# Output projection with bf16 operands in its two low products, and narrow copies made by GpSimd

## The reference, cut to what matters

```python
mlstm_out = jax.nn.sigmoid(o) * ht.reshape(bsz, s, V_W).astype(x.dtype)
mix = jnp.concatenate([conv_out, mlstm_out], axis=-1)
return x + jnp.einsum('bse,ed->bsd', mix, w_out)
...
logits = jnp.einsum('nd,de->ne', tokens.astype(jnp.float32), w_router.astype(jnp.float32))
affinity = jax.nn.softmax(logits, axis=-1)
gate, idx = lax.top_k(affinity.T, cap)
```

## Time and profile before

| | |
|---|---|
| runs of the kernel before | 1306.22, 1306.37, 1306.75 us; median 1306.37 |
| span of the profiled execution | 1307.2 us |
| TensorE busy | 1253.9 us, 96% |
| VectorE busy | 905.7 us, 69% |
| ScalarE busy | 742.0 us, 57% |
| GpSimd busy | 325.7 us, 25% |
| mean granted TensorE clock | 0.984 of full speed |
| the three products of L1965 | 66.7, 62.5 and 62.7 us busy, 160 matmuls each |

### The profile page before, as it was taken

The page is one execution under the profiler, slowest core; times in us unless marked ns, Lnnn a source line. Parts: engine busy times, 40 slices in busy tenths (PEclk is TensorE's granted clock), DMA queues, the critical chain, the costliest instruction groups (busy, mean ns, idle before and its releaser), DMA issues.

```text
span 1307.2 us, 25113 instructions
## 1 busy us (share of the span) xinstructions
PE 1253.9 (96%) x9762; PEld 1029.6 (79%) x9814; DVE 905.7 (69%) x1298; ACT 742.0 (57%) x1079; POOL 325.7 (25%) x316
## 2 busy tenths in 40 slices
PE   7999999999999999779999999999999999999992
PEld 6868986666687888568988898888888888888881
DVE  6462122541586655978888888888888889888985
ACT  7645322222345544447667766776676677667762
POOL 2512221010143231141133213221323132313040
PEclk9999999999999999989999999999999999999996
DMA  8231544361188763388999999999999999999894
GB/s 268 70 116 55 167 140 136 107 180 37 61 256 236 226 211 114 115 312 269 336 305 313 321 334 298 316 324 331 299 310 327 330 298 312 326 331 297 294 372 182
DMA packets 242032, 314.76 MB, mean 241 GB/s; under 512 B 16096, under 2 KB 206048, under 8 KB 241968
## 3 DMA queue, kind: packets, MB, share of 16 engines
q1 hardware_dynamic: 226576, 268.54, 62.2%
q0 software_dynamic: 15392, 45.36, 11.8%
HBM read 274.41 MB, written 39.44 MB: 240 GB/s over the span
## 4 chain that ended last, share of the span: by engine, by line
PE 89%; DMA 4%; DVE 3%; ACT 2%; issue 2%; SPq 1%; POOL 0%; DVEq 0%; ACTq 0%; POOLq 0%
PE psum L2253 23%; PE psum L2114 15%; PE psum L2260 11%; PE psum L2276 8%; PE psum L2081 8%; PE psum L1965 8%; PE psum L2294 4%; PE psum L2285 4%; PE psum L2246 1%; DMA eraw<-in_w_up_dram 1%; PE psum L2027 1%; ACT yt L1248 1%; DMA woraw<-in_w_out_dram 1%; PE psum L1987 1%; PE psum L1945 1%
## 5 line engine op out<-in xcount | busy, mean ns | idle before, releaser
L1812 DVE TENSOR_TENSOR elo<-eraw,ehi 128x2048 bf16<-128x2048 f32 x192 | 433.1, 2283 | 1.0 <-POOLq L822 1.0
L1218 ACT ACTIVATE ehi<-eraw 128x2048 fp32r<-128x2048 f32 x192 | 362.2, 1902 | 25.8 <-PE psum L2294 18.6
L2253 PE MATMUL psum<-xc,ehi 128*128 128x320 f32 x2048 | 332.4, 314 | 1.9 <-DVE xc L1817 1.9
L2253 PEld LDWEIGHTS psum<-xc,ehi 128*128 128x128 f32 x2048 | 304.2, 189 | 3.5 <-DVE xc L1817 2.3
L2260 PE MATMUL psum<-xb,elo 128*128 128x160 bf16 x2048 | 164.4, 234 | 0.0
L1825 DVE TENSOR_REDUCE gu<-psum 128x320 f32<-128x640 f32 x128 | 105.0, 820 | 82.6 <-PE psum L2260 82.5
L2260 PEld LDWEIGHTS psum<-xb,elo 128*128 128x128 bf16 x2048 | 139.0, 98 | 13.2 <-issue 0.2
L2114 PE MATMUL psum<-hn_nar,wnar 128*128 128x512 bf16 (+1 forms) x748 | 141.2, 343 | 1.2
L2276 PE MATMUL psum<-ehi,hc 128*128 128x512 f32 x512 | 132.6, 406 | 0.0
L2114 PEld LDWEIGHTS psum<-hn_nar,wnar 128*128 128x128 bf16 x768 | 73.0, 98 | 63.0 <-issue 4.5
L2276 PEld LDWEIGHTS psum<-ehi,hc 128*128 128x128 f32 x512 | 95.1, 188 | 22.2
(11 more groups left out here) (290 smaller groups left out, 1657.9 us busy)
## 6 DMA issues: line engine op xcount, KB each, us to landing
eraw<-in_w_gate_dram SPq DMA_DIRECT2D x64, 1024.0 KB, 6.3
eraw<-in_w_up_dram SPq DMA_DIRECT2D x64, 1024.0 KB, 8.9
eraw<-in_w_down_dram SPq DMA_DIRECT2D x64, 1024.0 KB, 13.3
wraw<-in_w_in_dram SPq DMA_DIRECT2D x12, 1024.0 KB, 7.5
negm<-negm_d SPq DMA_DIRECT2D x10, 512.0 KB, 7.2
acc_d<-x POOLq DMA_DIRECT2D x10, 512.0 KB, 5.4
tok_d<-tk POOLq DMA_DIRECT2D x10, 512.0 KB, 2.9
v<-v_d SPq DMA_DIRECT2D x18, 256.0 KB, 4.3
```

What stands on the lines that cost most here:

```text
L1218: act.activation(f["ehi"][:, j % RING, :], f["eraw"][:, raw_slot(s, j), :], ACT.Copy).then_inc(S["ehi"], 1)
L1812: dve.tensor_tensor(f["elo"][:, j % RING, :], f["eraw"][:, raw_slot(s, j), :], f["ehi"][:, j % RING, :].bitcast(F32), ALU.subtract).then_i ...
L2253: pe.matmul(o[:, 0:2 * NC], hi[:, k, c], x[:, k, :, :].rearrange("p a t -> p (a t)"), start=(k == 0), stop=False, skip_group_check=True)
```

## The change

The low halves and bf16 copies of the high halves now live together, in `mxn` and `won`, two bf16 planes (LOW and HIGH) in the place of the fp32r `mxl` and `wol`. VectorE's two subtractions write the LOW plane. GpSimd writes the HIGH plane: `out_weights_narrow(k)` copies a rounded weight slice (128x1024), behind the semaphore that its LOW plane has been written, because that plane's source lies in the same place; `mix_narrow(n, k0)` copies half of a tile's rounded mix (128x512), behind `mxh_done`. The high product stays fp32r; the two products with a low half take both operands in bf16. `project` gets the new waits: `wo_nar` for each k of the first tile, `mx_nar` ahead of k = 0 and of k = 4. In GpSimd's order the copies of weights 0 to 3 stand ahead of the last staging store, those of 4 to 7 between the first tile's two mix copies; in each turn one mix copy stands at the head and one behind `select_causal`.

```diff
-        for specs in ([("mxh", [P, KD, T], F32R), ("mxl", [P, KD, T], F32R)],
-                      [("woh4", [P, KD, T], F32R), ("wol4", [P, KD, T], F32R)],
+        for specs in ([("mxh", [P, KD, T], F32R), ("mxn", [P, KD, 2 * T], BF16)],
+                      [("woh4", [P, KD, T], F32R), ("won4", [P, KD, 2 * T], BF16)],
...
+            def out_weights_narrow(k):
+
+                pool.wait_ge(S["wo_lo"], k + 1)
+                pool.tensor_copy(out_narrow(k, HIGH), out_hi(k).bitcast(F32)).then_inc(S["wo_nar"], 1)
+
+            def mix_narrow(n, k0):
+
+                pool.wait_ge(S["mxh_done"], 2 * n + (1 if k0 == 0 else 2))
+                pool.tensor_copy(mxn[:, n % 2, HIGH, k0:k0 + 4, :], mxh[:, n % 2, k0:k0 + 4, :].bitcast(F32)
+                                 ).then_inc(S["mx_nar"], 1)
...
             for i in in_last[3:]:
+                if i == in_last[-1]:
+                    for k in range(4):
+                        out_weights_narrow(k)
                 store_group(i)
+            mix_narrow(0, 0)
+            for k in range(4, KD):
+                out_weights_narrow(k)
+            mix_narrow(0, 4)
             for n in range(NT + 2):
+                if 1 <= n < NT:
+                    mix_narrow(n, 0)
...
                     select_causal(n + 2)
+                if 1 <= n < NT:
+                    mix_narrow(n, 4)
...
-                dve.scalar_tensor_tensor(out_lo(k), out_raw(k), d["hgc"][:, k - 4:k - 3] if k >= 4 else 1.0,
+                dve.scalar_tensor_tensor(out_narrow(k, LOW), out_raw(k), d["hgc"][:, k - 4:k - 3] if k >= 4 else 1.0,
...
-                dve.tensor_tensor(mxl[:, s, 0:4, :], cvs[:, s, :, :], mxh[:, s, 0:4, :].bitcast(F32), ALU.subtract
+                dve.tensor_tensor(mxn[:, s, LOW, 0:4, :], cvs[:, s, :, :], mxh[:, s, 0:4, :].bitcast(F32), ALU.subtract
...
                     if n == 0:
                         pe.wait_ge(S["wo_lo"], k + 1)
+                        pe.wait_ge(S["wo_nar"], k + 1)
+                    if k0 == 0 and k == 0 and h == 0:
+                        pe.wait_ge(S["mx_nar"], 2 * n + 1)
                     if k == 4:
                         pe.wait_ge(S["mxl_done"], n + 1)
-                    xh, xl = mxh[:, n % 2, k, :], mxl[:, n % 2, k, :]
-                    wh, wl = out_hi(k)[:, c], out_lo(k)[:, c]
-                    for a, (x, w) in enumerate(((xh, wh), (xh, wl), (xl, wh))):
+                        pe.wait_ge(S["mx_nar"], 2 * n + 2)
+                    x, w = mxn[:, n % 2, :, k, :], [out_narrow(k, a)[:, c] for a in (LOW, HIGH)]
+                    for a, (x, w) in enumerate(((mxh[:, n % 2, k, :], out_hi(k)[:, c]), (x[:, HIGH, :], w[LOW]),
+                                                (x[:, LOW, :], w[HIGH]))):
```

More of the change, by code:

```diff
@@ L237, in hybrid_conv_mlstm_moe @@
         d.update(overlay(at_weights, ("woraw0", [P, 4, D], F32)))
-        d.update(overlay(at_weights, ("wol0", [P, 4, D], F32R)))
+        d.update(overlay(at_weights, ("won0", [P, 4, 2 * D], BF16)))
         d.update(overlay(at_weights + 2 * SLOT, ("woh0", [P, 2, D], F32R)))
@@ L264, in hybrid_conv_mlstm_moe @@
         mxh = d["mxh"][:, 2:4, SP_:T].rearrange("p s (k t) -> p s k t", k=KD)
-        mxl = d["mxl"][:, 0:2, SP_:T].rearrange("p s (k t) -> p s k t", k=KD)
+        mxn = d["mxn"][:, 0:2, 2 * SP_:2 * T].rearrange("p s (a k t) -> p s a k t", a=2, k=KD)
         cvs = d["cvs"][:, 1, SP_:T].rearrange("p (s k t) -> p s k t", s=2, k=4)
@@ L278, in out_hi, with out_narrow @@
             return d["woh4"][:, k, SP_:T]
-        def out_lo(k):
-            return d["wol0"][:, k, :] if k < 4 else d["wol4"][:, k, SP_:T]
+        def out_narrow(k, a):
+            return d["won0"][:, k, a * D:(a + 1) * D] if k < 4 else d["won4"][:, k, 2 * SP_ + a * D:2 * SP_ + (a + 1) * D]
         HALF2, PROMPT = 32, 64
@@ L338, in hybrid_conv_mlstm_moe @@
             "ld0 ld1 ldm0 ldm1 ld_mix0 ld_mix1 ld_x0 ld_x1 padded qs_done s_ps e_exp e_done sd_done num_ps router "
-            "den_done hb_done ht_done hsum mix_done mixT_ps mxh_done mxl_done o_ps x1_done "
+            "den_done hb_done ht_done hsum mix_done mixT_ps mxh_done mxl_done wo_nar mx_nar o_ps x1_done "
             "x1_out0 x1_out1 sum2 tk_done tk_out0 tk_out1 xT_ps2 xT_done "
@@ L1618, in heads_low @@
                 dve.wait_ge(S["mxh_done"], 2 * n + 2)
-                dve.tensor_tensor(mxl[:, n % 2, 4:8, :], psum[:, 5, :].rearrange("p (k t) -> p k t", k=4),
+                dve.tensor_tensor(mxn[:, n % 2, LOW, 4:8, :], psum[:, 5, :].rearrange("p (k t) -> p k t", k=4),
                                   mxh[:, n % 2, 4:8, :].bitcast(F32), ALU.subtract).then_inc(S["mxl_done"], 1)
```

## The result

The changed kernel takes **1321.37 us** (median of 4 runs, 1320.84 to 1322.50), the kernel before 1306.56 beside it. The ratio is 1.0115, with a 95% interval of 1.0102 to 1.0127. It is slower by 14.8 us, where I had forecast 8.0, and lies just above my range. The profiled execution has a span of 1319.2 us.

The account below looks back on a forecast made before the run. TensorE, busy for 96% of the span, was taken to bound the kernel. Start 4.1 + clock 1.4 + turn 2 1.0 + six turns 1.8 - tail 0.3 = +8.0 on 1306.4: 1314.4 us, range 1307.5 to 1320.5.

Parts of the forecast that it names:

- TensorE's gain: Output projection: triples with two bf16 products take 0.6725 instead of 0.685 us, saving 0.2 us a tile, 2.0 for ten.
- Place 1, the start: Start of the stage: TensorE waits at k = 4 for the mix cast behind the weight casts; cost 4.1 us (3.3 to 4.5).
- This alone would be harmless: Start: first four weight casts make the last staging store, first mix cast and first projection 1 to 2 us late, harmlessly.
- The clock: Start: after TensorE's idle stretches matmuls run at half speed for about 3.4 us; cost 1.4 us (0 to 2.9).
- Turn n = 2: Loop, tile 2: x has no room before the transposes, so the turn gets 1.0 us longer (0 to 1.6).
- Turns n = 3 to 8: Loop, six tiles: TensorE waits 0.35 to 0.75 us for x, less its gain: +0.3 each, 1.8 us together.
- With the two engines taking turns, two to four of the small operations each wait for a scaling: Loop: VectorE's inverse square root operations each wait for a 0.68 us GpSimd scaling; x comes 1.06 to 1.45 us late.
- or at 415.95 behind VectorE's conv subtraction: Loop: alternative start of GpSimd's four scalings, 415.95 instead of 415.45, if they wait for VectorE's conv subtraction.
- the signs that I had named: Loop: VectorE's small operations of 0.5 us or more, TensorE idle 0.3 to 0.8 at x's transposes, turns of 17.4 to 17.8.
- the whole-run hold: Loop: VectorE's chain to x held for the whole run of GpSimd's scalings, coming 1.85 us late.
- Heavier: Rival: VectorE held for the whole run of scalings, clock low for two stretches: +13.8 us, 1320.2; chance 0.15.
- Tail: Last turns, n = 9 and 10: no scalings there, so most of the gain is kept, -0.3 us.

Follow-up runs that it names:

- e3: Changed kernel without GpSimd's bf16 copies and the waits for them; TensorE takes bf16 low halves for both operands, leaving the cross products out: 1304.29 us.
- e6: e7 with ScalarE instead of GpSimd making the bf16 copies of weights 0 to 3: 1306.09 us.
- e7: e1 with GpSimd's cast of the heads half of the first mix ahead of the casts of weights 6 and 7: 1308.41 us.
- e1: Changed kernel with GpSimd's cast of the conv half of the mix behind the query scalings in the loop instead of ahead: 1312.22 us.
- e5: Changed kernel with the query scalings also waiting for VectorE's conv low halves: 1317.82 us.
- e8: Changed kernel with the conv half's cast and the DMA issue of the store of x swapped in GpSimd's loop: 1315.03 us.
- e9: Changed kernel with each of the four scalings waiting for the semaphore of the one before, leaving gaps between them: 1318.10 us.
- e4: Changed kernel with all casts kept, but TensorE using low halves for both operands and waiting for casts only at a tile's last products: 1319.48 us.
- e11: e6 with TensorE's k = 6 and 7 products last in tile 0, and ScalarE also making the copies of weights 6 and 7: 1305.75 us.

## Why the prediction was wrong, step by step

**TensorE's gain: right.** 0.2 us a tile forecast, 0.16 measured (17.24 to 17.08), with the bf16 pair at the pace I took from the input projection. The Trainium skill's 131 ns (page "TensorE: Matmul & The Clock Gate", Back-to-back issue gap), by which it would have been an estimated 30 us, doesn't hold in this kernel: e3 wins 1.8.

**Place 1, the start: right mechanism, 1.15 us short.** TensorE resumes at 386.47 where 387.5 less 2.09, 385.4, was forecast. The failed step is "This alone would be harmless", on the first four weight casts. I moved them in time only, and did not ask which operation of VectorE's they lie beside. They held the mix for 4.53 us, and with it the store and the low halves, and e6 against e7 puts 2.3 us on it.

**The clock: right**, 1.6 us in the changed kernel's trace (24 matmuls in 7.1 us instead of 5.5) against 1.4. It varies: e1, e5 and e8 have the same wait of 4.3 us but 6.8 us at half clock instead of 3.4, and e1's start is 1.1 us longer. 2.9 had been my upper bound.

**Turn n = 2: right**, +1.17 against +1.0, by the mechanism I named. Its scalings follow at 404.03, behind `conv_low`, and three small operations wait:

```profile
404.92 0.57 DVE L1346 TENSOR_SCALAR ms<-ms 128x5 f32<-128x5 f32 x1 [0.72 <-DVE nlm L1654]
405.52 0.64 DVE L1347 TENSOR_SCALAR ms<-ms 128x5 uint32<-128x5 uint32 x1
406.20 0.65 DVE L1350 TENSOR_TENSOR ms<-ms 128x5 f32<-128x5 f32 x1
```

**Turns n = 3 to 8: here it failed**, 1.16 a turn instead of 0.3, 5.2 us of the 6.8 missing. The step is "With the two engines taking turns, two to four of the small operations each wait for a scaling". I had placed the scalings right: 415.45 was forecast, and 421.20 less the 5.73 us by which this turn begins later (413.77 for 408.04) is 415.47. But I looked only at what would lie beside them *later on*. The operation that decides is the one that VectorE has in hand when they begin, `conv_low`, 0.13 us ahead. I had even used it ("or at 415.95 behind VectorE's conv subtraction"), as something that GpSimd might wait for, and never the other way round. The delay of x is then 2.1 us instead of 1.06 to 1.45, against a room of 0.83, which I had as 0.75 to 0.9. So 2.09 - 0.83 + 0.06 - 0.16 = 1.16. Of the signs that I had named, VectorE's small operations of 0.5 us or more didn't appear in these turns (0.17), the wait at the transposes of x was 1.1 us and not 0.3 to 0.8, and the turn 18.4 and not 17.4 to 17.8. What I forecast does exist: in e5, where it is alone, the turn is 17.80, 0.56 over the kernel before, just over the top of my range of 0.15 to 0.55.

I had the whole-run hold as "1.85" and in the rival *Heavier*, with the earlier trace rows as its only witness, and gave it 0.15. Its sum, 1320.2 us, is 1.2 from the result, but partly by luck: its terms for the clock (2.9, measured 1.6) and for turn 2 (1.5, measured 1.17) were too large and the one for the six turns (5.4, measured 7.0) too small. In the earlier trace rows VectorE's operation, from 354.90 to 359.70, outlasted not only the four scalings but the two selects behind them:

```profile
357.39 1.22 POOL L707 TENSOR_SCALAR_AFFINE_SELECT E<-E 128x512 f32<-128x512 f32 x2
```

I wrote of it that the trace agrees with the rule of the page. It agrees that the two exclude each other; the 3.56 us that the operation lost are five scalings' worth, not one. That single row was the best evidence there was on how long a hold lasts, and it spoke for the whole run, not for turns (the low half at 362.49, shown above, spoke for turns). I weighted it too low.

The Trainium skill, page "SBUF — State Buffer" (SBUF: two separate sides), says that whichever of the two instructions starts first gets the shared pair of ports "for the whole instruction" and the other fully blocks. By that a hold would last at most one scaling, 0.7 us, an estimate. The runs show such holds (small operations of 0.65 to 0.68 us instead of 0.17 in e5, `conv_low` of 0.88 in e8 and 1.43 in e9 instead of 0.68) and also holds of a whole run of GpSimd instructions (3.48 us instead of 0.68, 4.53 instead of 0.34, 4.80 instead of 1.24), and `conv_low`, which the profile shows starting first, went last. The measurement decides, and as an upper bound the run's length has to be taken.

**Tail: right**, -0.35 against -0.3.

Two small slips don't bear on this. The chances as split up add to 0.16 for the same and 0.79 for slower, not 0.17 and 0.78. And the median of the runs isn't 0.8 us below the span: the changed kernel's profiled execution has a span of 1319.2 us and a time of 1320.99, so a time is 1.8 above its span. By that the profiled execution of before took some 1309.0 us, 2.6 over the median (an estimate), to which the 2.09 above fits.

Summed by the medians of the runs: gain -1.8 (e3), start +7.9 (e1 over e3), loop order +8.7 (the changed kernel over e1, each against its own runs of before), together +14.8.

## What to carry to other kernels

A piece of work given to an idle engine is paid for where it stands in that engine's queue, not in its duration: the eighteen mix casts in the loop cost nothing that shows in e1, and 9 us when one of each pair stands ahead of the scalings. Before moving work between GpSimd and VectorE, list for every piece that shifts which operation of VectorE's is *already in hand* when it begins, and price that one with the length of GpSimd's whole run as upper bound. And compare the gain with one such meeting: here all of TensorE's gain, 1.8 us, is less than a single wait of 4.3.

## What the runs showed of the hardware beyond that

- A VectorE operation of 128x512 with two SBUF inputs took 3.48 us beside four back-to-back GpSimd scalings that directly followed a DMA issue of GpSimd's, 1.43 with gaps of 0.08 us between them, and 0.88 with a cast directly ahead of the row and the DMA issue 3.9 us ahead of it. One of 128x1024 took 4.80 us beside one such row and 1.75 beside another (1.24 alone).
- The start time that the profile gives of an operation of VectorE's doesn't tell whether it goes ahead of GpSimd's: `conv_low` is shown 0.13 us ahead of the scalings and comes in behind all four.
- An operation held off shows up as its own engine's busy time. VectorE's 70% instead of 69% of the span is such waiting: of the +23 us, 16 are the 2.73 us more in each of the six turns. A mean duration that moves between two traces of the same operation is the sign.
- Around an idle stretch of 4.3 us TensorE was granted half the clock (1.2 of 2.4 GHz) for 3.4 us in two executions (the changed kernel, e9) and 6.8 in three (e1, e5, e8). In the changed kernel the fall came 1 us behind the end of the stretch, in e1 still inside it. After idle stretches of 1.1 us (e7) and 2.6 (e4) it stayed full.
- A copy of 128x1024 from fp32r to bf16 takes 1.06 us on ScalarE (e11) and 1.04 on GpSimd undisturbed, up to 2.03 beside VectorE; the 128x512 cast takes 0.61, where I had estimated 0.55.
